# Weight loads and first loads in another order in a one-core decoder kernel: six expert pieces ahead of a ring, small loads on the ScalarE queue

## What is computed

```python
for l in range(DEPTH):                      # 2 layers
    xn = rmsnorm(h, g_attn[l])
    h = h + (mla(xn, ...) if l == 0 else swa_sink(xn, ...))
    xn = rmsnorm(h, g_ffn[l])
    h = h + (swiglu(xn, ...) if l == 0 else moe(xn, ...))
return rmsnorm(h, g_final)

def mla(xn, ...):
    lat = xn @ w_in                         # 1024 -> 384 + 256 + 64
    c_q = rmsnorm(lat[..., :384], g_q)
    c_kv = rmsnorm(lat[..., 384:640], g_kv)
    k_rope = rope(lat[..., 640:], positions)
    q = c_q @ w_uq; kv = c_kv @ w_ukv       # 8 heads
    ...
def moe(xn, w_router, w_gate, w_up, w_down):
    logits = xn @ w_router                  # 8 experts
    top_val, top_idx = lax.top_k(logits, 2)
    ...                                     # gates: softmax of the two
    hg = einsum('sd,edf->sef', xs, w_gate)  # 1024 x 3584 per expert
    hu = einsum('sd,edf->sef', xs, w_up)
    hh = silu(hg) * hu * gates
    return einsum('sef,efd->sd', hh, w_down)
```

## Time and profile before

| | us |
|---|---|
| median of 3 runs | 1253.48 |
| range of these | 1253.23 to 1255.0 |
| the profiled execution, its own time | 1255.29 |
| its span, first to last instruction | 1253.1 |
| mean granted TensorE clock | 0.995 |

### The profile page before, as it was taken

The page is one execution under the profiler, slowest core; times in us unless marked ns, Lnnn a source line. Parts: engine busy times, 40 slices in busy tenths (PEclk is TensorE's granted clock), DMA queues, the critical chain, the costliest instruction groups (busy, mean ns, idle before and its releaser), DMA issues.

```text
span 1253.1 us, 20363 instructions
## 1 busy us (share of the span) xinstructions
PE 1205.7 (96%) x8373; PEld 612.8 (49%) x8374; DVE 313.5 (25%) x710; ACT 262.8 (21%) x493; POOL 33.9 (3%) x55
## 2 busy tenths in 40 slices
PE   6999999999999999898999999999999999999996
PEld 4865777778765534333333433433343343334333
DVE  2355576667372400100110010010001101000101
ACT  2243433333263111011021101102101110211111
POOL 2100000000201100000000000000000000000001
PEclk9999999999999999999999999999999999999998
DMA  9612754436631799999999999999999999999994
GB/s 339 228 68 76 260 174 162 134 109 236 252 117 61 283 423 423 419 420 429 420 418 424 421 419 421 424 420 418 427 418 419 426 421 419 422 423 407 411 426 172
DMA packets 73164, 413.17 MB, mean 330 GB/s; under 512 B 6606, under 2 KB 11852, under 8 KB 64636
## 3 DMA queue, kind: packets, MB, share of 16 engines
q1 hardware_dynamic: 71996, 410.44, 80.9%
q0 software_dynamic: 944, 1.29, 0.3%
q10 hardware_dynamic: 144, 0.26, 0.1%
HBM read 410.91 MB, written 1.05 MB: 329 GB/s over the span
## 4 chain that ended last, share of the span: by engine, by line
PE 80%; DMA 11%; DVE 3%; issue 2%; ACT 2%; POOL 0%; SPq 0%; DVEq 0%; ACTq 0%; POOLq 0%
PE ps L1519 17%; PE ps L1499 11%; DMA ring<-in_moe_w_up 7%; PE ps L1494 6%; PE ps L1477 6%; DMA ring<-in_moe_w_down 4%; PE ps L1193 4%; PE ps L1189 4%; PE ps L1190 4%; PE ps L1481 3%; PE ps L1588 3%; PE ps L1552 3%; PE ps L1364 2%; PE ps L1155 2%; PE ps L1572 2%
## 5 line engine op out<-in xcount | busy, mean ns | idle before, releaser
L1519 PE MATMUL ps<-ring,arena 128*64 128x448 f32 x640 | 251.1, 545 | 8.1 <-issue 3.5
L1520 PE MATMUL ps<-ring,arena 128*64 128x448 f32 x640 | 251.2, 545 | 0.0
L1499 PE MATMUL ps<-ring,arena 128*32 128x448 f32 x1152 | 161.4, 539 | 0.0
L1519 PEld LDWEIGHTS ps<-ring,arena 128*64 128x64 f32 x640 | 84.5, 137 | 155.4 <-issue 141.5
L1500 PE MATMUL ps<-ring,arena 128*32 128x448 f32 x384 | 160.0, 539 | 0.0
L2066 DVE TENSOR_TENSOR arena<-arena,ps 64x448 f32<-64x448 f32 (+1 forms) x64 | 38.5, 614 | 368.9 <-ACT arena L955 190.5
L1588 PE MATMUL ps<-ring,arena 128*64 128x512 f32 x280 | 125.1, 596 | 4.7 <-DMA ring<-in_moe_w_down 4.7
L1589 PE MATMUL ps<-ring,arena 128*64 128x512 f32 x280 | 125.1, 596 | 0.0
L1494 PE MATMUL ps<-ring,arena 128*32 128x448 f32 x768 | 90.4, 542 | 6.5 <-DVE arena L2066 4.0
L1499 PEld LDWEIGHTS ps<-ring,arena 128*32 128x32 f32 x1152 | 48.0, 110 | 93.8 <-issue 93.8
L1813 DVE TENSOR_TENSOR w_lo<-ring,w_hi 128x2048 fp32r<-128x2048 f32 x33 | 75.6, 2292 | 60.0 <-ACT w_hi L841 58.5
(11 more groups left out here) (300 smaller groups left out, 1436.1 us busy)
## 6 DMA issues: line engine op xcount, KB each, us to landing
ring<-in_moe_w_down SPq DMA_DIRECT2D x64, 1792.0 KB, 20.9
ring<-in_moe_w_gate SPq DMA_DIRECT2D x127, 896.0 KB, 19.4
ring<-in_moe_w_up SPq DMA_DIRECT2D x127, 896.0 KB, 20.2
ring<-in_ffn_w_gate SPq DMA_DIRECT2D x5, 2048.0 KB, 7.8
ring<-in_ffn_w_up SPq DMA_DIRECT2D x5, 2048.0 KB, 8.0
ring<-in_ffn_w_down SPq DMA_DIRECT2D x5, 2048.0 KB, 8.1
ring<-in_mla_w_o SPq DMA_DIRECT2D x2, 2048.0 KB, 24.5
ring<-in_swa_w_q SPq DMA_DIRECT2D x2, 2048.0 KB, 8.4
```

The lines of the kernel that those rows point to most:

```text
L1499: pe.matmul(ps[32 * j:32 * j + 32, c, 0:CH], thirds[j], wu[:, c * CH:(c + 1) * CH], start=first, stop=last)
L1519: pe.matmul(ps[0:NARROW, c, 0:CH], lhs, wu[:, cols], start=(k == 0), stop=(k == KD - 1))
L1520: mm = pe.matmul(ps[64:64 + NARROW, c, 0:CH], lhs, wg[:, cols], start=(k == 0), stop=(k == KD - 1))
```

## The change

There are five parts.

1. **First loads.** SP issues the first half of x, then only the identity (128 of the 1275 columns of `consts`), then the second half of x, `win_q`, the rest of the constants, `win_kv` and the stream as before. The small vectors (eight loads in place of ten, since both rows of `g_attn` and of `g_ffn` now come in one) and the positions move to ACT's queue, ahead of its first instruction. PE's first wait is for the identity and the eight vectors; the positions have a semaphore of their own, and DVE takes them and the rope angles up behind the copies of the transposed rows. POOL fills its own exponents (`minus_half`) and doesn't wait for the constants.
2. **The norm's halves.** PE waits for each half of a transposed row tile before the four products that read it, not for both before the first. The transposes of `cq` move in between the two row tiles of `win_kv`, and DVE copies them out before it takes up the norm of the other latent.
3. **Six pieces ahead**: m = 22, 23 (set B, in `arena` where `hhT` lies) and m = 30, 31 (set A, behind it) are issued where m = 16, 17 were; m = 26, 27 (set C, in `xT2` and `xT`) behind m = 15 and two waits, for the last SWA output product and the router's. POOL copies B, C and A into the ring, each when its place has been read, and ACT waits for B's two copies before its item loop, since it writes `hhT` there. m = 16 and 17 are loaded into the ring like others. POOL issues the load of the final gain `gfin` behind the copies, since it goes into `xT2`.
4. **`swo0`** is released by the third output product in place of the fourth.
5. ACT's square of the SWA result writes its unused output into `xn`, and waits for it before it copies the rows there. The scratch of the routing tables lies in `hh`.

```diff
+        ysb = carve(D)
+        early = 12288 - 4 * PIECE
+        assert used[0] <= early
+        used[0] = early
         hhT = carve(2 * TILES * SLOTS, "p (a j n) -> p a j n", a=2, j=TILES)
-        ysb = carve(D)
...
-        AHEAD = (LAPS, LAPS + 1)
-        ahead = arena[:, 12288 - 2 * PIECE:12288].rearrange("p (a n) -> p a n", a=2)
-        assert used[0] <= 12288 - 2 * PIECE
+        AHEAD_B = {LAPS + 6: arena[:, early:early + PIECE], LAPS + 7: arena[:, early + PIECE:early + 2 * PIECE]}
+        AHEAD_C = {LAPS + 10: xT2[:].rearrange("p k n -> p (k n)")[:, 0:PIECE], LAPS + 11: xT[:].rearrange("p k n -> p (k n)")[:, 0:PIECE]}
+        AHEAD_A = {LAPS + 14: arena[:, early + 2 * PIECE:early + 3 * PIECE], LAPS + 15: arena[:, early + 3 * PIECE:early + 4 * PIECE]}
...
-            ("swo0", swo[:, :, 0:512], KD, 512, s.swo_mm, 4),
+            ("swo0", swo[:, :, 0:512], KD, 512, s.swo_mm, 3),
...
-            for t, landed in enumerate((s.x_loaded0, s.x_loaded1)):
-                sp.dma_start(h[:, t, :], x[0, t * P:(t + 1) * P, :]).then_inc(landed, 16)
...
-            sp.dma_start(cst[:], consts).then_inc(s.consts_loaded, 16)
-            for dst, src in loads:
-                sp.dma_start(dst, src, allow_slow_non_contiguous=dst.dtype == I32).then_inc(s.smalls_loaded, 16)
+            sp.dma_start(h[:, 0, :], x[0, 0:P, :]).then_inc(s.x_loaded0, 16)
+            sp.dma_start(ident, consts[:, C_ID:C_ID + P]).then_inc(s.ident_loaded, 16)
+            sp.dma_start(h[:, 1, :], x[0, P:2 * P, :]).then_inc(s.x_loaded1, 16)
...
+                if name == "win_q":
+                    sp.dma_start(cst[:, C_ID + P:C_N], consts[:, C_ID + P:C_N]).then_inc(s.consts_loaded, 16)
...
-                        for n, ma in enumerate(AHEAD):
-                            sp.dma_start(ahead[:, n, :], piece_of_expert(ma, expert)).then_inc(s.ahead_loaded, 16)
-                    if first and m in AHEAD:
+                        for ma, room in AHEAD_A.items():
+                            sp.dma_start(room, piece_of_expert(ma, expert)).then_inc(s.ahead_loaded_a, 16)
+                        for ma, room in AHEAD_B.items():
+                            sp.dma_start(room, piece_of_expert(ma, expert)).then_inc(s.ahead_loaded_b, 16)
+                    if first and m == LAPS:
+                        sp.wait_ge(s.swo_mm, 4)
+                        sp.wait_ge(s.router_mm, 2)
+                        for ma, room in AHEAD_C.items():
+                            sp.dma_start(room, piece_of_expert(ma, expert)).then_inc(s.ahead_loaded_c, 16)
+                    if first and (m in AHEAD_A or m in AHEAD_B or m in AHEAD_C):
                         continue
...
-            pool.wait_ge(s.consts_loaded, 16)
+            nc.gpsimd.memset(minus_half[:], -0.5).then_inc(s.pool_chain, 1)
+            pool.wait_ge(s.pool_chain, 1)
             rstd_rows()
...
-            pool.wait_ge(s.swo_mm, 4)
+            def take_ahead(rooms, landed, free, count):
+
+                pool.wait_ge(landed, 32)
+                pool.wait_ge(free, count)
+                for m, room in rooms.items():
+                    nc.gpsimd.tensor_copy(piece(m), room).then_inc(s.piece_landed[m % LAPS], 16)
+
+            take_ahead(AHEAD_B, s.ahead_loaded_b, s.gu_read, 5)
+            take_ahead(AHEAD_C, s.ahead_loaded_c, s.gu_read, 7)
+            take_ahead(AHEAD_A, s.ahead_loaded_a, s.gu_mm, 5)
+            for m in AHEAD_C:
+                pool.wait_ge(s.piece_landed[m % LAPS], 32)
             pool.dma_start(gfin, g_final.rearrange("(a n) -> a n", a=1).to_broadcast([P, D])).then_inc(s.rel_loaded, 16)
-
-            pool.wait_ge(s.ahead_loaded, 32)
-            pool.wait_ge(s.gu_read, 2)
-            for n, m in enumerate(AHEAD):
-                nc.gpsimd.tensor_copy(piece(m), ahead[:, n, :]).then_inc(s.piece_landed[m % LAPS], 16)
...
+            for dst, src in loads:
+                act.dma_start(dst, src).then_inc(s.smalls_loaded, 16)
...
+                act.wait_ge(s.ssq_ready, 7 + t)
                 act.copy(xn[:, t, :], h[:, t, :]).then_inc(s.xn_ready, 1)
...
+            for m in AHEAD_B:
+                act.wait_ge(s.piece_landed[m % LAPS], 32)
...
-            pe.wait_ge(s.consts_loaded, 16)
-            pe.wait_ge(s.smalls_loaded, 176)
+            pe.wait_ge(s.ident_loaded, 16)
+            pe.wait_ge(s.smalls_loaded, 16 * 8)
...
-                    pe.wait_ge(s.xT_ready, 2 * t + 2)
+                    if (name, t) == ("win_kv", 1):
+                        cq_T()
                     for k in range(KD):
+                        if k % 4 == 0:
+                            pe.wait_ge(s.xT_ready, 2 * t + 1 + k // 4)
...
-            dve.wait_ge(s.consts_loaded, 16)
-            dve.wait_ge(s.smalls_loaded, 176)
...
-            mean_squares(10, 6, KVL, 2, 2)
             dve.wait_ge(s.cT_mm, 1)
             for k in range(3):
                 dve.tensor_scalar(cqT[:, k, :], ps[:, k // 2, (k % 2) * S:(k % 2 + 1) * S], gcol(V_GQ, k), None, ALU.mult).then_inc(s.cqT_ready, 1)
+            mean_squares(10, 6, KVL, 2, 2)
```

More of the change, by code:

```diff
@@ L84 @@
 C_INV = C_THR + 1
-C_MH = C_INV + HALF
-C_KEY = C_MH + TT
+C_KEY = C_INV + HALF
 C_RANK = C_KEY + NE
@@ L770, in squares @@
                 act.activation(xn[:, t, :], h[:, t, :], ACT.Square, accum_out=stat[:, t:t + 1]).then_inc(s.ssq_ready, 1)
+            loads = [
+                (vecs[V_GA0:V_GA0 + 16, :], g_attn.rearrange("a (k n) -> (a k) n", n=P)),
+                (vecs[V_GF0:V_GF0 + 16, :], g_ffn.rearrange("a (k n) -> (a k) n", n=P)),
+                (vecs[V_KVG:V_KVG + 8, :], kv_g.rearrange("(k n) -> k n", n=P)),
+                (vecs[V_GQ:V_GQ + 3, :], g_q[0].rearrange("(k n) -> k n", n=P)),
+                (vecs[V_GKV:V_GKV + 2, :], g_kv[0].rearrange("(k n) -> k n", n=P)),
+                (vecs[V_KVB:V_KVB + 1, :], kv_b[0:P].rearrange("(k n) -> k n", n=P)),
+                (vecs[V_BQ:V_BQ + G, 0:HD], swa_b_q[0, 0:512].rearrange("(k n) -> k n", n=HD)),
+                (vecs[V_BQ:V_BQ + G, HD:P], swa_b_q[0, 512:1024].rearrange("(k n) -> k n", n=HD)),
+            ]
+            for dst, src in loads:
+                act.dma_start(dst, src).then_inc(s.smalls_loaded, 16)
+            act.dma_start(pos_i[:], positions[0].rearrange("(t p) -> p t", p=P), allow_slow_non_contiguous=True).then_inc(s.pos_loaded, 16)
             def square_half(t, half, done, count, junk):
@@ L942, in _ @@
                 act.wait_ge(s.h_attn1, 2 * t + 2)
-                act.activation(hhT[:].rearrange("p a j n -> p (a j n)")[:, 0:D], h[:, t, :], ACT.Square,
-                               accum_out=stat[:, t:t + 1]).then_inc(s.ssq_ready, 1)
+                act.activation(xn[:, t, :], h[:, t, :], ACT.Square, accum_out=stat[:, t:t + 1]).then_inc(s.ssq_ready, 1)
+                act.wait_ge(s.ssq_ready, 7 + t)
                 act.copy(xn[:, t, :], h[:, t, :]).then_inc(s.xn_ready, 1)
@@ L1039, in _, with cq_T @@
             rows_to_T(0, 1, 0)
+            def cq_T():
+                pe.wait_ge(s.cq_ready, 2)
+                for k in range(3):
+                    for t in range(TT):
+                        mm = pe.transpose(ps[:, k // 2, (k % 2) * S + t * P:(k % 2) * S + (t + 1) * P],
+                                          cq[:, t, k * P:(k + 1) * P], ident)
+                mm.then_inc(s.cT_mm, 1)
             for name, bank, n, sem in (("win_q", 4, QL, s.latq_mm), ("win_kv", 6, KVL + ROPE, s.latkv_mm)):
@@ L1049, in _ @@
                     mm.then_inc(sem, 1)
-            pe.wait_ge(s.cq_ready, 2)
-            for k in range(3):
-                for t in range(TT):
-                    mm = pe.transpose(ps[:, k // 2, (k % 2) * S + t * P:(k % 2) * S + (t + 1) * P],
-                                      cq[:, t, k * P:(k + 1) * P], ident)
-            mm.then_inc(s.cT_mm, 1)
             pe.wait_ge(s.cqT_ready, 3)
@@ L1680, in evac_xT @@
                         dve.tensor_tensor(o, src, g, ALU.mult).then_inc(s.xT_ready, 1)
-            dve.wait_ge(s.consts_loaded, 16)
-            dve.wait_ge(s.smalls_loaded, 176)
-            link(dve.tensor_copy(pos_f[:], pos_i[:]))
-            for t in range(TT):
-                link(dve.tensor_scalar(ang[:, 0, t, :], cst[:, C_INV:C_INV + HALF], pos_f[:, t:t + 1], None, ALU.mult))
             def reduced(dst, quarter):
@@ L1702, in _ @@
             evac_xT(0, 1, 0, xT, V_GA0)
+            dve.wait_ge(s.consts_loaded, 16)
+            dve.wait_ge(s.pos_loaded, 16)
+            link(dve.tensor_copy(pos_f[:], pos_i[:]))
+            for t in range(TT):
+                link(dve.tensor_scalar(ang[:, 0, t, :], cst[:, C_INV:C_INV + HALF], pos_f[:, t:t + 1], None, ALU.mult))
             reduced(4, 0.0)
```

38 lines of the change are left out of this document (15 added, 23 removed).

## The result

| | before | after |
|---|---|---|
| median of the runs, us | 1253.36 (4 runs, 1252.62 to 1255.0) | 1245.62 (4 runs, 1244.2 to 1246.49) |
| ratio of the times | | 0.9935, 95% interval 0.9923 to 0.9947 |
| the profiled execution, its own time | 1255.29 | 1246.03 |
| its span | 1253.1 | 1244.2 |
| mean granted TensorE clock | 0.995 | 0.996 |

The kernel is faster by 0.65%, some 8 us. The forecast was 1243.6, 2.0 us too low; the range of 1240.5 to 1248.0 holds the result.

A forecast was written before the change was run, and what follows sets the result against it. The DMA's bytes were taken to bound the expert loop, with PE a close second. Start 3.6, query latent 1.3 and loop 5.0 sum to 9.9 us, taken from the median 1253.5: 1243.6 us, range 1240.5 to 1248.0.

The forecast's parts named there:

- The bound: Expert loop: one long DMA transfer near 420 GB/s sets its end; PE, waiting 9.1 us for pieces, is a close second.
- The start, 3.6 us to the first product: Opening loads and norm: PE's first product comes at 11.7 instead of 15.51, 3.8 us earlier, taken as 3.6.
- The rival of late small loads: Start: ACT issues slower, or loads land behind x and `win_q`; gain 1 us, not 3.6; 1246.2 us; chance 0.12.
- The query latent, 1.3 us: Between `win_kv`'s two tiles: transposing `cq` there hides its copy out, which kept PE waiting 1.36 us; 1.3 us earlier.
- Start and latent together, 4.9 us: Ahead of the loop: the start's 3.6 and the query latent's 1.3 us; all that stays if the loop's gain is absorbed.
- The loop, 5.0 us: Expert loop: six pieces ahead gain 6.2 us, less 1.2 for the final gain's load; 5.0 us, capped at 6.6.
- The final gain's 1.2 us: Loop's stream: the 0.52 MB load, free before, now goes into the full stream and loses 1.2 us.
- `swo0` as C's cover: Ahead of the loop: early release worth nothing itself; without it C would end near 426, not about 420.
- The copies: First item: POOL's pairs take 3.29 us each, with over 20 us available; nothing in sum.
- the ports: First item's half: a 1.65 us copy blocks DVE's products, delaying PE and the ring's opening; rival at 1245.2 us, chance 0.04.
- the rival of a slower loop: Loop head: a 3.5 us PE idle recurs at six other returns, 21 us; 1260.5 us; chance 0.03.
- The down weights: First expert: issued about 5 us before 454.58, DMA idle just before, then full from about 451 to 1220.

The follow-up runs named there:

- swo4: The changed kernel with `swo0` released by the fourth output product again: 1245.27 us, ratio 0.9930.
- hold_win: The changed kernel with SP waiting for the eight small loads before it issues `win_q`: 1246.87 us, a single run.
- gfin_end: The changed kernel with the final gain issued by SP behind the last expert's pieces: 1245.02 us, ratio 0.9931.
- loop_only: The kernel before plus parts 3, 4 and 5 only, the start as before: 1249.14 us, ratio 0.9961.
- vec_late: The changed kernel with the first tile's rows transposed before the small vectors, which get their own PSUM bank: 1245.23 us, ratio 0.9932.
- start_only: The kernel before plus parts 1 and 2 only, the loop with two pieces ahead as before: 1249.62 us, ratio 0.9965.
- no_c: The changed kernel without set C, so four pieces ahead, and the final gain loaded early: 1245.27 us, ratio 0.9928.
- gfin_late: The changed kernel without set C, so four pieces ahead, the final gain still behind POOL's last copy: 1246.29 us, ratio 0.9940.

## Why the prediction came out as it did

- **The bound.** Right. The DMA is full through the loop and PE's waits for pieces shrink only where it catches the DMA, between 500 and 620 us. The pieces at later wide items' ends are as late as before: 9.1 - 6.6 = 2.5 us of waits outside that window before, 5.5 - 3.2 = 2.3 now. `swo4` adds that 1.6 us of PE's time in the second item don't reach the end.
- **The start, 3.6 us to the first product.** Right in the middle, with more spread than I gave it. Four of nine executions have it at 12.0 (3.5 us), one at 12.6, and four at 13.2 to 13.3 (2.2 us), as the small loads land at 7.9 to 9.2, not 7.4. The step that was mis-sized is their landing: I took it from the positions' row, which stood ahead of `win_q` in the queue and not behind it, and `hold_win` shows that this matters by 0.9 us and more. ACT's issues were sized too low as well (nine in 3.6 us and not 3.15, the square at 5.59 and not 5.1), which the landing hid. The rival of late small loads was thus half true in half of the executions, and the times hardly show it. The term also took PE's first product as worth its full time: PE runs at 1.2 GHz until the clock's first entry, and up to 1.3 us of an early start go there (`gfin_end`). The sum had no term for it.
- **The query latent, 1.3 us.** Right, if a little small: 1.36 us by the wait, 1.4 by the times, 1.5 by the traces with the clock's part taken off.
- **Start and latent together, 4.9 us.** First `w_uq` product at 37.64 (mean of `before` and `loop_only`), 32.9 (median of eight traces with both parts, the two with `vec_late`'s order aside): 4.8 us. `start_only` gives 4.4 by its time.
- **The loop, 5.0 us.** 4.6 in the traces, by terms that both fail and cancel. The gain of the pieces was taken as 6.2 us, from a down stream that would be full 1.4 us behind its issue; the step left out that the stream then runs with one or two requests under way, as their rooms come free, and by `gfin_end` and `no_c` 1.5 us are lost there (1.2 of them in the low rates). The final gain's 1.2 us were then subtracted, and they cost next to nothing, since they move in a gap that is there anyway. For a stream without the gap `no_c` and `gfin_late` show that the load does cost, 2.1 us in one trace of each and not 1.2.
- **`swo0` as C's cover.** Wrong in what hangs on it. C did end late without it, as worked out, but C's landing 6.3 us late costs nothing, and C itself is worth nothing. The text valued six pieces by bytes and then capped them by the down weights' room; counted for four pieces as well, that cap would have shown that they nearly reach it.
- **The copies, ACT's wait, the ports, the rival of a slower loop.** Right: 3.30 us for each pair, six or more microseconds apart, no wait of PE for any; the single wait of 3.3 us at the loop's head stands there once, as before. DVE's four products beside a copy take 605 to 614 ns, the others 612 in the median, so no row shows DVE held up by one; the rule of the Trainium skill that the prediction weighed (SBUF — State Buffer, Who interferes with whom) has it so too for products with one input in PSUM.
- **The down weights.** Said 5 us ahead of 454.58, measured 4.4; the idle DMA just before (7 GB/s) and the end of the stream at 1219 as said. PE's waits in 500 to 620 us are 3.2 us and not 1 to 2, since the gain ended at 4.6.
- **The 2 us of the miss.** The steps, by traces, add up to 4.8 + 4.6 = 9.4 us of the 9.9. By the times the gain is 8.1 to 8.3, with an interval of 1.7 either way. The predicted span was 1243.2, and the median span of nine executions of the changed kernel is 1243.8. So the step that failed is the last one, the base: the profiled execution of before has a span of 1253.1, and 27 others have a median of 1251.4 (1250.2 to 1253.2), so gains read from one of the longest executions were subtracted from a median of shorter ones; from its own time they give 1255.3 - 9.9 = 1245.4. One place in which executions differ could be named: in the gather ahead of the loop the granted clock of some, of either kernel, is at 0.5 (1.2 GHz) for some three microseconds, in others it stays at 1.00 and PE has 1.0 us of idle time there, and the way from the first `w_uq` product to the down weights is 416.6 to 416.9 or 416.2 to 416.4 us. The profiled execution of before has the dip. That is 0.5 us of the 1.7. Another is the clock at the start: its first entry is 2.3 us behind the first product in that execution, which costs 1.15 us, and the other executions of before were not traced. An estimate goes further. From the first `w_uq` product on the traces agree: 416.2 to 416.9 us to the down weights, the loop, and 12.2 us from the last scatter product on. With these the median span of 1251.4 puts the first `w_uq` product of before near 36.5 and not at 37.64, and the changed kernel's 1243.8 puts its own near 33.5. Start and latent would then give some 3 us between typical executions and not 4.8, and the steps 7.6, as the spans do; it is worked back from the spans and no test of them. So most of the miss would be a start that was read from a late execution; no trace of a typical one is there to show it.

## What to carry to other kernels

Prefetching ahead of a saturated stream pays only until the next place where the stream is paced by freed room; count pieces one pair at a time and stop at that place, since whatever is further ahead is handed back there, and a small load moved into such a gap is free. A reordering whose wait stands in the trace with its length (here 1.36 us) can be taken at face value. A start that waits for small loads should be sized with the large loads beside them, and its first products at the pace they have in the trace: a clock column of 1.00 says nothing of a stretch for which the trace has no entry. And where one execution is profiled, gains read from it are worth the difference to its own time, not to a median that it doesn't represent.

## What was not expected of the hardware

- The same eight small loads, asked for at the same times, landed at 7.9 or at 9.2 us, and at 7.0 with the large ones held back.
- TensorE's clock reached 2.4 GHz between 12.1 and 15.5 us in nine executions with the same order of the start. Until then a product of `w_in` took its place every 0.64 us, behind it every 0.32 us, and up to 1.3 us were lost.
- A fall of the clock to 1.2 GHz for some three microseconds, behind 3.3 us of idle time at the loop's head, came in some executions and not in others, and cost nothing, since PE waits for the DMA later on.
- One or two requests of 1.8 MB under way don't fill the DMA: with down issues 3.9 us apart and 4.4 us of bytes in each, the rate was 258 to 315 GB/s for four windows, not 420.
